# Output gates, three merge products and the feed-forward part joined into one queue per engine

## The reference, cut to what matters

```
z = rmsnorm(x, norm1_g) @ w_in                    # q, k, v, mLSTM q, k, v, om, gates ga, gb
o_att = three dilated window attentions, merged by the softmax of their log-sums
h_m   = mLSTM memory read, chunk by chunk          # and for the samples from a stored state
ya = o_att @ w_att_out                             # 512 -> 1024
yb = (sigmoid(om) * h_m) @ w_m_out                 # 1024 -> 1024
x  = x + (sigmoid(ga) * ya + sigmoid(gb) * yb) @ w_o
h  = rmsnorm(x, norm2_g)
y  = x + (silu(h @ w_gate) * (h @ w_up)) @ w_down  # 1024 -> 2816 -> 1024
```

## Time and profile before

| | us |
|---|---|
| median of three runs | 2319.31 |
| the profiled execution | 2320.55 |
| its span in the profile | 2318.8 |
| PE busy | 2208.5 (95%) |
| DVE, ACT, POOL busy | 966.0, 509.5, 679.6 |
| mean granted clock of PE | 0.979 |

### The profile page before, as it was taken

The page is one execution under the profiler, slowest core; times in us unless marked ns, Lnnn a source line. Parts: engine busy times, 40 slices in busy tenths (PEclk is TensorE's granted clock), DMA queues, the critical chain, the costliest instruction groups (busy, mean ns, idle before and its releaser), DMA issues. The chain is left out here.

```text
span 2318.8 us, 33929 instructions
## 1 busy us (share of the span) xinstructions
PE 2208.5 (95%) x13646; PEld 2066.1 (89%) x13646; DVE 966.0 (42%) x1831; ACT 509.5 (22%) x1111; POOL 679.6 (29%) x662
## 2 busy tenths in 40 slices
PE   5899999999999999999788988989999999999999
PEld 4677999999977778999787988979999999999998
DVE  5765774476134322333364533243332222333224
ACT  3312553354233213333111011021000000000001
POOL 4224222231122312222231243432443323443310
PEclk9999999999999999999899999999999999999999
DMA  6435244434467736554577562613333223332202
GB/s 222 130 104 191 101 160 160 161 130 157 157 207 256 249 127 200 191 192 159 163 272 227 176 232 84 199 55 100 109 96 100 76 68 108 109 110 91 91 28 74
DMA packets 201274, 337.55 MB, mean 146 GB/s; under 512 B 39798, under 2 KB 112310, under 8 KB 198422
## 3 DMA queue, kind: packets, MB, share of 16 engines
q1 hardware_dynamic: 141624, 269.49, 35.7%
q10 hardware_dynamic: 59494, 65.90, 8.7%
HBM read 262.45 MB, written 160.94 MB: 183 GB/s over the span
## 5 line engine op out<-in xcount | busy, mean ns | idle before, releaser
L272 POOL CAST whi<-raw 128x512 fp32r<-128x512 f32 x324 | 248.0, 766 | 1521.1 <-PE ps L2011 521.0
L274 POOL TENSOR_TENSOR wlo<-raw,whi 128x512 fp32r<-128x512 f32 x324 | 439.3, 1356 | 32.8 <-issue 6.9
L285 PE MATMUL ps<-whi,hhi 128*128 128x512 f32 x832 | 346.2, 416 | 1.2 <-ACT zt L627 1.0
L286 PE MATMUL ps<-wlo,hhi 128*128 128x512 f32 x832 | 333.4, 401 | 0.0
L287 PE MATMUL ps<-whi,hlo 128*128 128x512 f32 x832 | 333.3, 401 | 0.0
L2011 PE MATMUL ps<-h2hi,whi 128*128 128x344 f32 x1056 | 225.4, 322 | 10.3 <-DVE h2lo L2567 8.9
L285 PEld LDWEIGHTS ps<-whi,hhi 128*128 128x128 f32 x832 | 208.3, 250 | 21.2 <-ACT zt L627 1.5
L287 PEld LDWEIGHTS ps<-whi,hlo 128*128 128x128 f32 x832 | 208.1, 250 | 20.6
L286 PEld LDWEIGHTS ps<-wlo,hhi 128*128 128x128 f32 x832 | 209.5, 252 | 18.4
L2011 PE MATMUL ps<-h2lo,whi 128*128 128x344 f32 x1056 | 224.2, 320 | 0.0
L2011 PE MATMUL ps<-h2hi,wlo 128*128 128x344 f32 x1056 | 223.5, 320 | 0.0
(11 more groups left out here) (326 smaller groups left out, 3326.7 us busy)
## 6 DMA issues: line engine op xcount, KB each, us to landing
out<-in_cache_kv_w SPq DMA_DIRECT2D x144, 512.0 KB, 4.8
raw<-in_w_in SPq DMA_DIRECT2D x152, 256.0 KB, 4.4
a_tr<-tt SPq DMA_DIRECT2D x48, 256.0 KB, 2.0
out<-in_cache_kv_w SPq DMA_DIRECT2D x24, 508.0 KB, 5.0
raw<-in_w_gate SPq DMA_DIRECT2D x88, 128.0 KB, 2.2
raw<-in_w_up SPq DMA_DIRECT2D x88, 128.0 KB, 2.3
raw<-in_w_down SPq DMA_DIRECT2D x44, 256.0 KB, 3.7
gates<-e_sg ACTq DMA_DIRECT2D x16, 516.0 KB, 5.5
```

Of the source, the lines that this page charges most:

```text
L272: pool.tensor_copy(self.whi[:, p % RING, :], self.raw[:, p % RAW, :]).then_inc(self.w_hi, 1)
L274: pool.tensor_tensor(self.wlo[:, p % RING, :], self.raw[:, p % RAW, :], self.whi[:, p % RING, :].bitcast(F32), ALU.subtract).then_inc(self ...
L285: nc.tensor.matmul(out, lhs[0], rhs[0], start=start, stop=False)
L286: nc.tensor.matmul(out, lhs[0], rhs[1], start=False, stop=False)
```

## The change

The five blocks become one (`layer_end`), in which each engine runs one queue; the classes `OutputGates`, `Products` and `Ffn` hold the stages' parts. In words:

- Row tiles of an input lie in two tiles of four rows each (`xs[0]`, `xs[1]`, hi and lo together), used by all stages. `operand(k)` gives hi and lo of row tile k. When PE has passed row tile k with the last unit of a stage (each such unit counts `w_used` per tile), ACT casts the next stage's row tile k into the same place and DVE takes the rest.
- The attention rows stay in SBUF (`at`); `att_t` is gone. The eighth unit of the gates waits for the finished merge and softmax, and runs as one unit of three banks with one sigmoid of 1032 columns.
- All rows (sigmoid(ga), sigmoid(gb), `hm_t`, x) are loaded by ACT. The ring `rw` has four slots, used by 8 gate rows, 7 memory rows and 8 gate rows in turn; memory row 3 goes to a spare tile, memory row 4 comes last, into the slot of the eighth gate row.
- SP issues the sample's loads when all of the gates' stores have landed (`over`), and the remaining weights behind them. The samples' small results are stored one unit earlier, and the states' stores are spread.
- Small tiles (masks, rope table, statistics) share one tile `misc`, whose space later serves as row buffers.
- In attention, the scores of two neighbouring key tiles that lie in neighbouring slots are one matmul of 256 columns in place of two of 128.

```diff
+    def left(self, eng, stage, k):
+        eng.wait_ge(self.core.w_used, self.p0[stage] + self.nk[stage] + k + 1)
...
+    def act_attention(self):
+        gates.merged(act)
+        for k in range(4):
+            act.wait_ge(core.w_used, gates.p0 + KD + k + 1)
+            self.cast(k, gates.at[:, k, :])
...
+    def act_memory(self, k):
+        src, e = self.memory_row(k)
+        if e is None:
+            act.wait_ge(self.h3_in, 16)
+        else:
+            self.row_loaded(act, e)
+        if k < 4:
+            self.left(act, 0, k)
+        elif k == 4:
+            act.wait_ge(self.sample.up, NB)
+        self.cast(k, src)
...
+        for k in range(4):                      # end of act_first
+            self.act_memory(k)
+            if k:
+                self.load_row(11 + k)
+        self.load_row(11)
+        for k in range(4, KD):
+            self.act_memory(k)
+        sample.act_store(6)
+        sample.act_store(7)
...
+    def dve_first(self):
+        for u in range(KD):
+            if u == 7:
+                for k in range(3):
+                    self.dve_memory(k)
+            self.complete(dve, u)
+            self.row_loaded(dve, u)
+            dve.tensor_tensor(seg3(self.acc[:, u, :]), self.banks(u), seg3(self.rw[:, u % self.RING, :].bitcast(F32)),
+                              ALU.mult).then_inc(self.ev, 1)
+            if u == 7:
+                self.dve_memory(3)
+                self.dve_memory(4)
+            sample.dve(u)
+        dve.wait_ge(sample.std, 4 * NB)
+        for k in range(5, KD):
+            self.dve_memory(k)
...
+    def act_second(self):
+        for e in range(2 * KD - 1, 3 * KD - 1):
+            self.load_row(e)
+        for k in range(KD):
+            self.left(act, 1, k)
+            act.wait_ge(self.ev, KD + k + 1)
+            self.cast(k, self.acc[:, k, :])
+        for k in range(KD):
+            act.wait_ge(self.xl, 4 + KD + k + 1)
+            act.dma_start(self.acc[:, k, :], core.x_t[k]).then_inc(self.x_in[k // 2], 16)
...
+        for u in range(KD):                     # dve_third
+            if u == KD - 1:
+                normed(0)
+                add_squares(KD - 2)
+                for k in range(1, KD - 1):
+                    normed(k)
+            self.complete(dve, 2 * KD + u)
+            dve.wait_ge(self.x_in[u // 2], 32)
+            dve.tensor_tensor(seg3(acc[:, u, :]), seg3(acc[:, u, :]), self.banks(2 * KD + u), ALU.add).then_inc(self.ev, 1)
...
+        normed(KD - 1)
+        add_squares(KD - 1)
...
+        @block.sync                             # layer_end
+        def _(sp):
+            core.load_weights(products.p0[1] + 3)
+            gates.over(sp)
+            products.sample.load()
+            core.load_weights(core.taken)
+            ffn.sp()
...
+                if slots in ([0, 1], [1, 2]):   # scores
+                    last = pe.matmul(ps[:, 3 + par, at:at + 2 * P].rearrange("p (b c) -> p b c", b=2), query,
+                                     self.k[rows, slots[0]:slots[1] + 1, h // 2, :], start=True, stop=True)
+                    continue
```

More of the change, by code:

```diff
@@ L390, in act @@
             act.wait_ge(self.hi, 2 * (NT + 1))
-            act.activation(core.hs[:, :, 0:NB], core.hhi[:, :, S:T], ACT.Copy).then_inc(self.hs, 1)
+            for half in range(2):
+                act.activation(core.hs[:, 4 * half:4 * half + 4, 0:NB], core.xs[half][:, 0, :, S:T],
+                               ACT.Copy).then_inc(self.hs, 1)
     def dve(self, n):
@@ L575, in pe @@
                     continue
-                lhs = [residues(a[:, k, 0:S], 0 if g == "m" else g, n) for a in (core.hhi, core.hlo)]
+                lhs = [residues(a[:, 0:S], 0 if g == "m" else g, n) for a in core.operand(k)]
                 if n == 0:
@@ L813, in pe @@
                 rows = slice(DH * par, DH * par + DH)
[L814 to L817, removed]
+                query, at, slots = self.q[rows, N % 2, h // 2, :], 2 * j * P, [(g * NT + m) % 3 for m in self.blocks(g, n)]
+                if slots in ([0, 1], [1, 2]):
+                    last = pe.matmul(ps[:, 3 + par, at:at + 2 * P].rearrange("p (b c) -> p b c", b=2), query,
+                                     self.k[rows, slots[0]:slots[1] + 1, h // 2, :], start=True, stop=True)
+                    continue
+                for b, slot in enumerate(slots):
+                    last = pe.matmul(ps[:, 3 + par, at + b * P:at + (b + 1) * P], query, self.k[rows, slot, h // 2, :],
+                                     start=True, stop=True)
             last.then_inc(self.qk, 1)
@@ L2336, in _ @@
+            core.load_weights(products.p0[1] + 3)
[3 more added lines that the diff above has]
+            ffn.sp()
         @block.gpsimd
         def _(pool):
-            core.split_weights(core.taken + 8)
+            gates.pool()
+            core.split_weights(core.taken)
+        @block.tensor
+        def _(pe):
+            gates.pe()
+            products.pe_first()
+            products.pe_second()
+            products.pe_third()
+            ffn.pe()
@@ L2340, in _ @@
         @block.scalar
         def _(act):
-            for k in range(KD):
-                nc.scalar.activation(hi[:, k, :], acc[:, k, :], ACT.Copy).then_inc(his, 1)
-            for u in range(KD):
-                act.wait_ge(ev, u + 1)
-                if u >= 2:
-                    act.wait_ge(sum_sq, u - 1)
-                nc.scalar.activation(sq[:] if u else core.ssq[:], acc[:, u, :], ACT.Square).then_inc(sqd, 1)
+            gates.act()
+            products.act_attention()
+            gates.act_last()
@@ L2361, in _ @@
-            for u in range(KD):
-                units.wait(dve, u)
-                dve.wait_ge(x_in[u // 2], 32)
-                nc.vector.tensor_tensor(seg3(acc[:, u, :]), seg3(acc[:, u, :]), banks(core, u), ALU.add).then_inc(ev, 1)
-                if u >= 2:
-                    add_squares(u - 1)
-            add_squares(KD - 1)
-        @block.tensor
-        def _(pe):
-            for u in range(KD):
-                if u >= 2:
-                    pe.wait_ge(ev, u - 1)
-                units.product(pe, u, (hi, lo), los)
```

954 lines of the change are left out of this document (500 added, 454 removed).

## The result

The changed kernel takes **2304.7 us** (median of 5 runs, 2298.3 to 2308.4) beside 2319.3 for the kernel before; the ratio is 0.9932 with the interval [0.9912, 0.9953], so 11 to 20 us less. A second series gave 2304.4 and 0.9926 [0.9906, 0.9946]. The forecast was 2291 in 2278 to 2305: the sign held and the median lies inside the range, by 0.3 us only, but of the 29 us only 15 came. In the profiled pair it is 19 (2320.55 to 2301.42).

The account below looks back on a forecast made before the run. PE, busy 95%, was taken as the bound, with 43.8 us at stake at four seams. 44 less 16.9 remaining is 27, plus 2 from scores: 29 off 2319.3 is 2290.3, stated as 2291, range 2278 to 2305.

Parts of the forecast that it names:

- 31.8 us of pauses: PE's idle time at four stage starts, waiting for the low part of the input: 9.8, 8.25, 5.97 and 7.76 us.
- 12.0 of half speed: Time PE was taken to lose running matmuls at 1.2 instead of 2.4 GHz behind the pauses at the four seams.
- Memory product and output projection: Seam into the memory product: 7.8 us in place of 12.1, mostly waiting for tile 4; seam into the projection: 1 us.
- Gates to attention product: Seam cost 6.6 us in place of 11.4: 0.8 for merge and softmax, 4 stall on r_z, 1.8 half speed.
- Projection to feed-forward: Last seam: PE waits for the rest of tile 7, 1.5 us, bounds 0 and 5.
- Scores: Merged score matmuls in 14 attention items save 0.16 us each, 2 us in all, bounds 0 and 7.7.
- A: Rival: nearly everything hidden, r_z and memory row land as fast as the store; gain 40.6, 2279 us; chance 0.13.
- B: Rival: loads decide; r_z 8 plus 2.3, states 5 later, tile 4 costs 13; gain 14, 2305 us; chance 0.17.
- C: Rival: every VectorE rest runs under a GpSimd weight split, 2.2 us each; gain 21, 2298 us; chance 0.14.
- D: Rival: slower; half speed for two units at each seam, four seams costing 74 us; 2347 us; chance 0.03.
- The signs named: Expected trace marks: r_z and fifth-tile waits, clock 1.00 at last two seams; wrong if seam idle exceeds 25 us.

## Why the prediction was right in sign and off in size

- **What bounds it, 31.8 us of pauses and 12.0 of half speed.** Right for the pauses: PE idled 16.0 us less in the stretch, and with the casts of three seams late all of the gain was gone. The half speed did not pay: of the 12.0 the sum left 3.6, so 8.4 were to come back, and PE's busy time fell by 0.6 (330.1 to 329.6). Some 3.0 of the 12.0 were small pauses that I had read as half speed (94.81 less 93.78 and 93.89 less 93.11 in the earlier trace rows, 1.2 in the first unit of the feed-forward part). Of the rest, the memory product and the projection gave back 3.0 as busy time (186.9 to 183.9), and the attention product took 3.4 more (68.8 to 72.1).
- **Memory product and output projection.** Right to 0.1 us as a sum. The tile wait was 6.3 and 0.4 and, with some 15 matmuls at half speed, 8.7 where 7.8 was forecast; the seam to the projection was clean where 1 was forecast. The sum is partly luck. By the forecast's count, from the end of unit 7 at 1335.9, the row of the fifth tile left at +4.0 where +3.7 was forecast (1339.90, the second of the two issues in the first timeline line below). But it took 7.7 us to land (the DMA line of that issue), not 4.6 to 6.4, so PE waited 6.3 instead of 4.1; the sixth tile, put at 1.9 of wait, cost 0.4. A cache copy had left SP 1.9 us ahead of this row as well; no run takes that one away, so its share is open.

```profile
rw<-hm_t ACTq DMA_DIRECT2D x1, 516.0 KB, 7.7
```

```profile
1338.75 1.47 ACTq L2315 DMA_DIRECT2D rw<-hm_t  x2
1347.60 1.06 ACT L2327 ACTIVATE x_c<-rw 128x1032 fp32r<-128x1032 f32 x1 [9.59 <-DMA rw<-hm_t]
1348.70 1.24 DVE L2332 TENSOR_TENSOR x_c<-rw,x_c 128x1032 fp32r<-128x1032 f32 x1 [7.04 <-ACT x_c L2327]
1350.08 2.06 PE L2012 MATMUL ps<-x_c,whi 128*128 128x344 f32 x6 [6.33 <-DVE x_c L2332]
```

- **Gates to attention product: the step that failed.** "r_z leaves at +5.4 ... 4 us of stall, and 1.8 for half speed". It left at +8.8 and the stall was 9.2, with 2.5 of half speed: 5.9 of the 8.3 us missed in this part. I priced the store by the quiet store of the earlier trace rows, 2.9, and charged the crowd to r_z alone. The store met it first: SP issues the cache copies along with the weight pieces, and two of them now left 6.5 and 0.7 us ahead of the store, which I had not placed. Another 2.0 lie in the 64 state products, 10.85 us instead of 8.8; but with the scores alone, whose code here is that of before, they took 10.88 at a clock of 0.64, as in the changed kernel, and in the profile of before 8.85 at 0.80. So this is most likely that one profile and no cost of the change; two profiles of this code are too few to show it. The rest, 0.4, stays unexplained.
- **Projection to feed-forward.** Forecast 1.5, measured 2.0 of pause, and half speed that I had put at nothing:

```profile
1538.09 1.16 ACT L2327 ACTIVATE x_c<-acc,g 128x1032 fp32r<-128x1032 f32 x1 [9.71 <-DVE acc L2495]
1539.28 1.29 DVE L2484 SCALAR_TENSOR_TENSOR x_c<-acc,g,x_c 128x1032 fp32r<-128x1032 f32 x1 [1.28 <-ACT x_c L2327]
1540.72 1.33 PE L2012 MATMUL ps<-x_c,whi 128*128 128x344 f32 x6 [2.04 <-DVE x_c L2484]
1541.85 1.06 PE L2012 MATMUL ps<-x_c,wlo 128*128 128x344 f32 x3
1542.96 2.98 PE L2617 MATMUL ps<-misc,ones 128*128 128x344 f32 x6
```

  Rest 7 ends at +12.1, not +10.7: the square's sum took 2.3 and the six rests behind it 1.8 to 2.0 each beside the splits, so VectorE was through at +8.4 where +6.5 was forecast. Behind the pause of 2.04 the last tile's nine matmuls took 2.2 us instead of 1.4, and the six of the sum 2.98 instead of 1.90: 1.9 of half speed.
- **Scores.** 1.8 in the items, against 2; not told apart from nothing by the time.
- **The rivals.** A (all hidden) fell at r_z. B had the right place and nearly the right sum for the attention seam (8 and 2.3 forecast, 9.2 and 2.5 found), and the time it gave, 2305, is the median; but it asked 5 for the states and 13 for tile 4, of which neither came. C is real, and smaller than it was put. D did not occur: no seam ran a whole unit at half speed; the longest stretch at half speed behind a pause was 18 matmuls, behind r_z. The measured median lies at the edge of my range: 8.3 of the 10.4 us missed in the stretch come from one seam, where 14.1 us (9.2 of stall, 2.5 of half speed, 2.0 for the state products and 0.4) stand in place of 5.8. That it lies inside, by 0.3 us, where the ratio's interval is 10 us wide, is luck as much as judgement, and that it equals B's 2305 is chance.
- **The signs named.** The r_z wait was to be 2 to 8 and was 9.2; the tile wait, 3 to 6, was 6.3; the idle sum at the seams was 18.8, below the 25 that would have meant failure; the clock at the last seam was 0.91, not 1.00, and 0.98 from the memory product to the projection's end. The part ahead moved by 1.2 us, within the 5 named.

## What to carry to other kernels

Rounding the next stage's input under the last unit of this one was worth 15 us at three seams here, as much as the whole change; joining the queues is what makes it possible, and what it is worth by itself was not measured. When a seam closes, look for the transfer that used to land inside it, and place every other transfer that the new order sets beside it, on all queues, the ones that ride along with weight loads too. Then move the consumer rather than speed the load (in the stretch, one number in the code was worth 10.2 us, the edits of the traffic 3.4 to 6.1), and let the slot that comes free last hold the row that is needed last (6.2 us).

## What was not expected of the hardware

A 64 KB load took 2.6 us from issue to use with only such traffic behind it, 5.2 beside four rows of 516 KB issued 3.5 us earlier on another queue, and 6.4 with a cache copy also about; a 512 KB store took 2.9, 3.8 and 5.5 in the same three cases. With the copy and without the rows the load took 3.2 and the store 6.3. Each of these is one profile. And the same 64 products of 2 columns took 8.8 to 13.7 us over fourteen profiles, with the granted clock: 8.8 at 0.80, 10.2 at 0.69, 10.9 at 0.64 and 13.7 at 0.51. What set the clock there was not looked into; a stretch of such tiny matmuls varies by more than several of the edits were worth.
